# MLA attention on one Trainium2 core: the values of an even round move behind the scores and turns of the next

## The reference

```python
def dense_attention(q, k, v, scale):
    s = jnp.einsum('bqhd,bkhd->bhqk', q, k).astype(jnp.float32) * scale
    p = jax.nn.softmax(s, axis=-1).astype(v.dtype)
    return jnp.einsum('bhqk,bkhd->bqhd', p, v)

# even_layer
a_l = blocked_dense_attention(q_l, jnp.concatenate([k_c, k_l], axis=1),
                              jnp.concatenate([v_c, v_l], axis=1), MLA_SCALE)
y_l = jnp.concatenate([fourier_mix(f_in) * jax.nn.silu(f_gate),
                       a_l.reshape(b, n, MLA_WIDTH) * jax.nn.silu(m_gate)], axis=-1) @ w_out
a_c = dense_attention(q_c, k_c, v_c, MLA_SCALE)
```

## Time and profile before

| What | us |
|---|---|
| Median of three runs | 1078.01 (1077.76 to 1079.28) |
| The profiled execution, its own time | 1077.22 |
| Its span | 1075.2 |
| TensorE busy (PE) | 1046.4, 97% |
| VectorE busy (DVE) | 682.3, 63% |
| ScalarE busy (ACT) | 553.5, 51% |
| The MLA attention, first scores to first projection product | 817.2 to 869.0 |

### The profile page before, as it was taken

The page is one execution under the profiler, slowest core; times in us unless marked ns, Lnnn a source line. Parts: engine busy times, 40 slices in busy tenths (PEclk is TensorE's granted clock), DMA queues, the critical chain, the costliest instruction groups (busy, mean ns, idle before and its releaser), DMA issues.

```text
span 1075.2 us, 15602 instructions
## 1 busy us (share of the span) xinstructions
PE 1046.4 (97%) x5974; PEld 876.8 (82%) x5974; DVE 682.3 (63%) x1201; ACT 553.5 (51%) x1002; POOL 77.8 (7%) x95
## 2 busy tenths in 40 slices
PE   7999999999999999999999999999998999999997
PEld 6899777788887999777788788899986678889785
DVE  6995766666546895765666457433457734976664
ACT  6564465555436564464655346234336643543772
POOL 1000110000002000110000000001000002120040
PEclk9999999999999999999999999999999999999999
DMA  9655577766666655586866575133231021542001
GB/s 335 209 159 160 194 237 233 244 196 189 196 195 236 207 154 169 186 283 214 282 213 181 204 282 150 51 101 107 75 98 37 2 79 40 165 154 93 2 1 40
DMA packets 109845, 170.73 MB, mean 159 GB/s; under 512 B 7246, under 2 KB 70747, under 8 KB 109515
## 3 DMA queue, kind: packets, MB, share of 16 engines
q1 hardware_dynamic: 107668, 161.95, 47.2%
q0 software_dynamic: 1568, 6.37, 1.8%
q10 hardware_dynamic: 534, 1.41, 0.3%
HBM read 168.19 MB, written 1.05 MB: 157 GB/s over the span
## 4 chain that ended last, share of the span: by engine, by line
PE 85%; DVE 8%; ACT 2%; issue 2%; DMA 1%; POOL 0%; SPq 0%; DVEq 0%; POOLq 0%; ACTq 0%
PE PS L482 16%; PE PS L487 16%; PE PS L483 15%; PE PS L3041 4%; PE PS L3045 4%; PE PS L3042 4%; PE PS L989 2%; DVE low L452 2%; PE PS L1841 2%; PE PS L950 1%; PE PS L951 1%; PE PS L955 1%; PE PS L1829 1%; PE PS L1952 1%; PE PS L999 1%
## 5 line engine op out<-in xcount | busy, mean ns | idle before, releaser
L452 DVE TENSOR_TENSOR low<-raw,high 128x1024 fp32r<-128x1024 f32 (+3 forms) x182 | 202.1, 1116 | 171.6 <-ACT high L442 170.3
L482 PE MATMUL PS<-high,hT_high 128*128 128x512 f32 (+2 forms) x796 | 302.2, 380 | 0.4 <-ACT high L442 0.3
L483 PE MATMUL PS<-high,hT_low 128*128 128x512 f32 (+2 forms) x796 | 295.1, 371 | 0.0
L442 ACT ACTIVATE high<-raw 128x1024 fp32r<-128x1024 f32 (+3 forms) x186 | 179.4, 972 | 209.6 <-PE PS L487 114.2
L487 PE MATMUL PS<-low,hT_high 128*128 128x512 f32 (+2 forms) x796 | 231.2, 371 | 1.0 <-DVE low L455 1.0
L482 PEld LDWEIGHTS PS<-high,hT_high 128*128 128x128 f32 x796 | 149.8, 188 | 33.2 <-issue 8.6
L487 PEld LDWEIGHTS PS<-low,hT_high 128*128 128x128 f32 x796 | 146.9, 188 | 23.6 <-DVE low L455 2.4
L483 PEld LDWEIGHTS PS<-high,hT_low 128*128 128x128 f32 x796 | 149.9, 188 | 19.4
L455 DVE SCALAR_TENSOR_TENSOR low<-raw,vec_cols,high 128x512 fp32r<-128x512 f32 x176 | 123.6, 747 | 66.2 <-ACT high L445 66.1
L445 ACT ACTIVATE high<-raw,vec_cols 128x512 fp32r<-128x512 f32 x176 | 117.1, 715 | 62.7 <-PE PS L487 32.0
L3041 PE MATMUL PS<-high,fT_high 128*128 128x512 f32 x176 | 69.5, 395 | 0.0
(11 more groups left out here) (372 smaller groups left out, 1584.2 us busy)
## 6 DMA issues: line engine op xcount, KB each, us to landing
raw<-w_gate_up SPq DMA_DIRECT2D x176, 256.0 KB
raw<-w_mod SPq DMA_DIRECT2D x48, 512.0 KB
raw<-w_down SPq DMA_DIRECT2D x44, 512.0 KB
raw<-w_in SPq DMA_DIRECT2D x56, 384.0 KB
raw<-o_w_in SPq DMA_DIRECT2D x20, 512.0 KB
raw<-w_out SPq DMA_DIRECT2D x16, 512.0 KB
raw<-e_w_in SPq DMA_DIRECT2D x12, 512.0 KB
raw<-w_in SPq DMA_DIRECT2D x8, 512.0 KB
```

Source lines behind the costliest of these rows:

```text
L442: last = e.activation(g.high, g.raw, ACT.Copy)
L452: last = e.tensor_tensor(g.low, g.raw, g.high.bitcast(F32), ALU.subtract)
L482: e.matmul(bank, xh[:, k, tokens], g.high[:, i, :], start=first and i == 0, stop=False)
L483: e.matmul(bank, xl[:, k, tokens], g.high[:, i, :], start=False, stop=False)
```

## The change

Two rounds are taken in one turn of the loop. The order was S(p) T(p-1) V(p-2) S(p+1) T(p) V(p-1), with S for scores, T for turns and V for values; it becomes S(p) T(p-1) S(p+1) T(p) V(p-2) V(p-1), for even p. The waits of each piece stay as they were, and the ScalarE, VectorE and POOL code isn't touched.

```diff
-            for p in range(pairs + 2):
+            def scores(p):
+                for i in (2 * p, 2 * p + 1):
+                    if i >= 4:
+                        e.wait_ge(act.sem, act.value(f"mla_exp{i - 4}"))
+                    mla_scores(*mla_steps[i], PS[:, MLA_SCORES[i % 4], :]).then_inc(pe.sem, pe.mark(f"mla_scores{i}"))
+
+            def turns(p):
+                for j in (2 * p, 2 * p + 1):
+                    e.wait_ge(dve.sem, dve.value(f"mla_weights{j}"))
+                    if j >= 2:
+                        mla_copied(e, j - 2)
+                    else:
+                        e.wait_ge(dve.sem, dve.value(f"ye_L{j}"))
+                    for b in range(mla_steps[j][2]):
+                        last = e.transpose(PS[:, 2 + j % 2, b * P:(b + 1) * P], mla_prob[:, j % 4, b * P:(b + 1) * P], ident)
+                    last.then_inc(pe.sem, pe.mark(f"mla_turned{j}"))
+
+            def values(q):
+                if q in (0, 4):
+                    e.wait_ge(dve.sem, dve.value(f"ye_L{2 + q // 4}"))
+                elif q % 4 == 0:
+                    e.wait_ge(dve.sem, dve.value(f"ya_F{q // 4 - 2}"))
+                blocks = mla_steps[2 * q][2]
+                for b in range(blocks):
+                    for m in (2 * q, 2 * q + 1):
+                        mla_copied(e, m)
+                        h, t, _ = mla_steps[m]
+                        last = e.matmul(mla_out(mla_bank(h // 2), h, t), mla_value(h, b), probT_late[:, m % 4, b, :],
+                                        start=b == 0, stop=b == blocks - 1)
+                last.then_inc(pe.sem, pe.mark(f"mla_values{2 * q + 1}"))
+
+            for p in range(0, pairs + 2, 2):
                 if p < pairs:
...
+                    scores(p)
+                if p:
+                    turns(p - 1)
+                if p < pairs:
+                    scores(p + 1)
+                    turns(p)
+                if p:
+                    values(p - 2)
+                    values(p - 1)
```

More of the change, by code:

```diff
@@ L1751, in mla_attention_pe @@
                 ye_turn_pe(e, u)
-            for p in range(pairs + 2):
-                if p < pairs:
[L1754 to L1781, removed]
```

## The result

The changed kernel takes **1083.19 us** (median of six runs, 1082.71 to 1083.73) against 1078.05 for the kernel before; ratio 1.0051, 95% interval 1.004 to 1.0061. A second set of runs gave 1082.58 us and 1.0042 (1.0029 to 1.0055). It is slower, as forecast, but by some 5 us where 3.1 were forecast, and 1083.19 lies above the range's upper end of 1082.7.

What follows compares the result with a forecast made beforehand. The loop of VectorE and ScalarE was taken to set the pace, with TensorE 0.59 us to spare per head pair. Late scores (0.86 us) and copy waits summed to 3.07 us slower, 1081.1 us, range 1077.2 to 1082.7 us.

Steps and rivals of the forecast that it cites:

- What bounds the kernel: Attention stage: VectorE and ScalarE's loop sets the pace, 12.39 us per head pair; TensorE alone needs 11.80.
- Point 1: TensorE's own time: each joined pair of value groups saves 0.32 us, seven pairs 2.2 us, costed at nothing.
- values-to-values: TensorE's boundary between two joined groups of values: between 0 and 0.28 us, taken as 0.
- turns-to-scores: TensorE's boundary where scores follow turns at once: a gap of 0.05 us.
- Point 2: ScalarE's copy waits for late values: 0.68 us three times, 0.03 twice (p = 8, 12), 0.11 at p = 4.
- point 4: Later work doesn't catch up: the exponential behind a delayed copy starts later by the same time; the shift goes through.
- W: End of VectorE's weights of a step, the last thing the loop does in a round; delays are counted from it.
- Point 3: Scores of round 4 stand behind a second wide group of values, so they and the loop move 0.86 us later.
- The sum: Whole change: 0.86 + 0.11 + 0.03 + 0.03 + 3 x 0.68 = 3.07 us slower.
- Rival C: Worse: values-to-values costs 0.28 us and six later hand-overs 0.2 us more each, 4.6 us slower, 1082.6 us; chance 0.04.
- A: Rival: TensorE is the bound after all, so the seven savings count, faster at about 1075.6 us; chance 0.13.
- B: Rival: ScalarE's new wait bites less or is half taken up, 1078.9 or 1080.0 us; chance 0.26.

Runs made afterwards that it cites:

- join_all_but_first_act: Values joined everywhere but in the first pair, plus both ScalarE exponentials of a round ahead of both copies: 1076.81 us, ratio 0.9986 to the kernel before.
- before_act_order: Kernel before the change, with both ScalarE exponentials of a round put ahead of both copies: 1078.14 us, ratio 0.9999 to the kernel before.
- join_first_only: Kernel before, with only round 0's values moved behind the turns of round 2: 1079.85 us, ratio 1.0013 to the kernel before.
- fill_gap: Changed kernel plus 13 identity transposes in TensorE's empty stretch: 1081.88 us, ratio 1.0033 to the kernel before; again 1081.21 us, 1.003.
- join_all_but_first: Changed kernel, but round 0's values stay ahead of the scores of round 3, as before: 1080.45 us, ratio 1.0021 to the kernel before.
- v_before_turns: Against the changed kernel, even-round values go behind the next scores but ahead of the next turns: 1078.36 us, ratio 1.0001 to the kernel before.
- after_act_order: Changed kernel, with both ScalarE exponentials of a round put ahead of both copies: 1077.81 us, ratio 0.9996 to the kernel before.

## Why the prediction was right in direction and wrong in size

*What bounds the kernel.* Right. The loop of VectorE and ScalarE set the pace: maxima 13.07 us apart instead of 12.40, TensorE less busy.

*Point 1, TensorE's own time.* Right that the gain buys nothing here, and right in its size: the turns ahead of scores take 0.44 us instead of 0.53, two wide groups of values 1.90 instead of twice 1.02, and scores behind turns 1.72 to 1.75 instead of 1.82, together 0.30 to 0.33 us a pair. The boundary values-to-values costs nothing, turns-to-scores 0 instead of 0.05. That joining is worth something once the loop is out of the way shows in join_all_but_first_act, whose attention is 1.6 us shorter than before_act_order's.

*Point 2, the new wait.* Right in place, near in size: 0.60, 0.61 and 0.59 us instead of 0.68, and 0.10 us at p = 8 and 12 instead of 0.03. The step behind the 0.68 was half wrong, and it was point 4's "starts later by the same time". The copy of step 12 started 1.63 us after W (843.73 to 845.36), later than the 1.55 taken. But the next exponential followed it by 0.28 us, where before it was 0.46 (845.36 to 845.64 above; 853.45 to 853.91 in the trace of before):

```profile
853.91 0.47 ACT L1868 ACTIVATE z_late<-PS,stats 128x256 f32<-128x256 f32 x1
```

*Point 3, the late scores.* Right for the work: 0.86 us in the profile of join_first_only in which the clock was kept.

*The sum.* 3.07 us, and 3.12 us in fill_gap's profile, where the clock is kept. As a count of waits it held, but that the two are so close is partly luck: 0.23 us of the 3.12 are the VectorE loss under "A small one", which the sum doesn't have, and the waits themselves came to 2.89.

*The step that failed* is the speed that point 3 took for granted. It costed the 16 further records of values, and all work around them, at the rate of the steady rounds (2 x 0.43 us) and put a change of the clock at nothing, without a reason. I followed the values of round 0 to where they went and asked who waits for them, but not what they left: TensorE idle for 1.57 us between the scores of round 3 and the turns of round 2, and behind it the joined values of rounds 0 and 1, on the path, at half clock. The clock is worth 1.56 us (2.42 less 0.86) in the profile shown, and the clock fell in all three profiles of the changed kernel. No rival had it. Rival C, the only one on that side, put its extra in the hand-overs, of which nothing came, and that is where the upper end of 1082.7 came from.

*A small one.* I costed POOL at nothing. In the changed kernel its transfer of the context is issued while VectorE multiplies by the weights of step 29:

```profile
869.29 0.75 POOL L2077 DMA_DIRECT2D kT<-ctx  x1 [56.70 <-PE PS L1964]
```

```profile
869.33 0.16 DVE L1897 RECIPROCAL stats<-stats 128x1 f32<-128x1 f32 x1 [0.39 <-ACT z_late L1880]
869.53 0.61 DVE L1900 TENSOR_SCALAR z_late<-z_late,stats 128x256 f32<-128x256 f32 x1
```

That multiplication took 0.61 us, the same one elsewhere 0.35, and it stands in the loop: the 0.23 us of round 14. Before, the transfer was issued at 865.61, beside work of VectorE that reads PSUM. The other profiles agree. The issue overlaps the multiplication of step 29 in seven of the fourteen (the changed kernel's three, fill_gap's two, join_all_but_first and v_before_turns), and it took 0.61 us in all seven; in the other seven it fell beside other work, and the multiplication took 0.35. The rows of v_before_turns, whose 0.17 us over before are accounted for by this:

```profile
865.33 0.75 POOL L2083 DMA_DIRECT2D kT<-ctx  x1 [52.78 <-PE PS L1970]
```

```profile
865.55 0.61 DVE L1906 TENSOR_SCALAR z_late<-z_late,stats 128x256 f32<-128x256 f32 x1
```

So the overlap and the longer multiplication go together throughout. Why isn't shown, and no run moved the transfer by itself.

*Rivals.* A fell with the 13.07 us. The Trainium skill, "TensorEngine Tiling (Array Packing)", Key Properties, says that a change of the tiling mode drains the engine. The rows agree as far as that goes: of every two runs of 64-column products one goes, and with it some 0.3 us of TensorE's time. It says nothing of who waits. B fell with the three 0.7 us waits in ScalarE's rows.

## What to carry to other kernels

Before work is moved to save an engine time, find out whether that engine sets the pace, by the distance from start to start of its rounds and not by its busy share; and look for what the moved work frees, since a buffer released late can stop an in-order engine with its most urgent work behind it. If so, put the waiting item last on that engine: here one order on ScalarE turned 5 us of loss into none. And look at the hole that moved work leaves on TensorE, for behind it the clock may be at half.

## What the runs showed of the hardware that I had not expected

An idle stretch of 1.57 us on TensorE, and one of up to 0.51 us a turn later, went with the clock at 1.2 GHz in four of five profiles with that stretch as it stands in the change; the 32 value records then took 2.9 to 3.6 us to the next start instead of 1.9. With 13 transposes in the hole the clock stayed at 2.4 GHz in both profiles. The same kernel can do either from one execution to the next (join_first_only, 52.66 and 55.27 us), and after_act_order kept it behind 2.19 us of idle time in its one profile. The Trainium skill, "TensorE: Matmul & The Clock Gate", Part 1, says that the chip's window of observation runs free of the kernel; these runs agree that the same program can fall on either side, and show nothing of the window itself.

VectorE's multiplication of 128x256 values took 0.61 us instead of 0.35 in every profile in which POOL's issue of a transfer (0.75 us) overlapped it, seven of seven. Its work that reads PSUM kept its time beside the same issue (0.68 us for the gating at 865.26 before).
